# The first group's C and x0 inside the modulation stream, and the second modulation's sets one group later

## The reference

```python
mx = modulation(c, ada_w, ada_b)          # silu(c) @ ada_w + ada_b, split in 6 of 2048
hx = modulate(rms_norm(x, norm_g[0]), mx[0], mx[1])      # first modulation: shift, scale
yx, _ = ssd_mixer(hx, hc, w_in, conv_w, ..., w_out)      # hc: the same of ctx with c_ctx
x = x + mx[2] * yx
hx = modulate(rms_norm(x, norm_g[1]), mx[3], mx[4])      # second modulation
x = x + mx[5] * hier_moe(hx)              # top-1 group of 4, top-2 expert of 8

# ssd_mixer
z, xbc, dt = split(h @ w_in, [4096, 4096 + 6144])        # xbc: x 4096, B 1024, C 1024
xbc = silu(conv3(xbc)); dt = softplus(dt + dt_bias)      # 64 heads, two directions
# per direction: chunked scan, y = C (decays) B x, context first, then latent
y = rms_norm((y_fwd + y_bwd + d_skip * x) * silu(z), norm_g) @ w_out
```

## Time and profile before

| what | us |
|---|---|
| median of 3 runs (2125.37 to 2130.33) | 2125.74 |
| the profiled execution | 2125.82 |
| its span, first to last instruction | 2124.3 |
| TensorE busy | 1958.4 (92%) |
| VectorE busy | 1229.8 (58%) |
| ScalarE busy | 496.5 (23%) |
| GpSimd busy | 153.7 (7%) |
| DMA, mean over the span | 308 GB/s |

### The profile page before, as it was taken

One profiled execution on the slowest core, in us unless ns is written; L12 is line 12 of the kernel. 1 busy time (PEld: TensorE's weight loads), 2 busy tenths in 40 slices (PEclk: granted clock), 3 DMA queues, 4 the chain that ended last, 5 costly groups with the idle time before them and its releaser, 6 DMA issues.

```text
span 2124.3 us, 27901 instructions
## 1 busy us (share of the span) xinstructions
PE 1958.4 (92%) x10096; PEld 1213.4 (57%) x10097; DVE 1229.8 (58%) x2010; ACT 496.5 (23%) x577; POOL 153.7 (7%) x214
## 2 busy tenths in 40 slices
PE   5778999999999999999987999988999998899897
PEld 2357888888888888877876433333333333333332
DVE  2457898989999998988875433222332232333224
ACT  3233434343434243444443200000000000000000
POOL 0000010101000000002961000000000000000000
PEclk9789999999999999999998999999999999999999
DMA  9958577768686868596745699999999699999996
GB/s 360 317 162 266 173 237 213 240 182 267 183 256 179 255 188 249 174 334 244 257 165 218 275 426 428 425 426 425 427 429 425 255 426 426 425 428 426 425 427 274
DMA packets 293597, 654.10 MB, mean 308 GB/s; under 512 B 13408, under 2 KB 187904, under 8 KB 260912
## 3 DMA queue, kind: packets, MB, share of 16 engines
q1 hardware_dynamic: 284608, 626.86, 79.0%
q0 software_dynamic: 7984, 26.40, 3.8%
q10 hardware_dynamic: 960, 0.23, 0.1%
HBM read 642.81 MB, written 10.65 MB: 308 GB/s over the span
## 4 chain that ended last, share of the span: by engine, by line
DMA 27%; PE 19%; POOL 4%; DVE 1%; issue 1%; SPq 1%; ACT 0%; DVEq 0%; POOLq 0%
DMA wt<-in_moe_w_up 27%; PE bank L1875 13%; PE bank L1730 2%; POOL ysq L648 2%; POOL ysq L655 1%; PE bank L1900 1%; POOL ysq L653 1%; PE bank L1855 1%; SPq L536 1%; PE bank L1837 0%; PE bank L1838 0%; PE bank L1789 0%; PE bank L1782 0%; PE bank L1830 0%; DVE x L1502 0%
## 5 line engine op out<-in xcount | busy, mean ns | idle before, releaser
L1875 PE MATMUL bank<-wt,xe 128*64 128x512 f32 x1984 | 465.2, 624 | 75.8 <-DMA wt<-in_moe_w_up 75.8
L1502 DVE TENSOR_TENSOR x<-x,bank 128x512 f32<-128x512 f32 x256 | 158.5, 682 | 528.4 <-PE bank L1855 528.4
L1623 PE MATMUL bank<-hTh,whi 128*128 128x256 f32 (+1 forms) x1264 | 408.5, 343 | 9.5 <-ACT whi L716 6.6
L1624 PE MATMUL bank<-hTl,whi 128*128 128x256 f32 (+1 forms) x1264 | 401.9, 338 | 0.0
L1875 PEld LDWEIGHTS bank<-wt,xe 128*64 128x64 f32 x1984 | 162.7, 144 | 374.9 <-issue 374.9
L1623 PEld LDWEIGHTS bank<-hTh,whi 128*128 128x128 f32 x1264 | 242.9, 192 | 37.1 <-ACT whi L716 6.8
L1624 PEld LDWEIGHTS bank<-hTl,whi 128*128 128x128 f32 x1264 | 242.8, 192 | 24.1
L1630 PE MATMUL bank<-hTh,wlo 128*128 128x256 f32 (+1 forms) x1264 | 231.3, 336 | 0.9 <-DVE wlo L967 0.9
L1900 PE MATMUL bank<-wt,hdn 128*64 128x512 f32 x1024 | 226.8, 596 | 1.4 <-DVE hdn L1514 1.4
L879 ACT ACTIVATE gsb<-bank 128x512 f32<-128x512 f32 x32 | 19.1, 597 | 828.5 <-PE bank L1875 828.5
L1630 PEld LDWEIGHTS bank<-hTh,wlo 128*128 128x128 f32 x1264 | 196.9, 190 | 25.3 <-DVE wlo L967 1.1
(11 more groups left out here) (316 smaller groups left out, 1834.8 us busy)
## 6 DMA issues: line engine op xcount, KB each, us to landing
wt<-in_moe_w_gate SPq DMA_DIRECT2D x62, 2048.0 KB, 16.6
wt<-in_moe_w_up SPq DMA_DIRECT2D x62, 2048.0 KB, 21.1
wt<-in_moe_w_down SPq DMA_DIRECT2D x62, 2048.0 KB, 18.5
raw<-in_ssm_w_in SPq DMA_DIRECT2D x80, 1024.0 KB, 5.8
raw<-in_ada_w SPq DMA_DIRECT2D x70, 1024.0 KB, 6.1
raw<-in_ssm_w_out SPq DMA_DIRECT2D x32, 1024.0 KB, 5.1
fr<-in_ada_w SPq DMA_DIRECT2D x26, 1024.0 KB, 12.0
bc<-cum_d POOLq DMA_DIRECT2D x32, 512.0 KB, 5.3
```

Of the source, the lines that this page charges most:

```text
L1502: dve.tensor_tensor(x1[:, tt, cols], x1[:, tt, cols], banks[(1, 3, 6, 7)[nb]][:, :], ALU.add).then_inc(s_acc2, 1)
L1623: pe.matmul(bank[:, 0:width], wh[:, k, :], hTh[:, k, 0:width], start=(k == 0), stop=False)
L1624: last = pe.matmul(bank[:, 0:width], wh[:, k, :], hTl[:, k, 0:width], start=False, stop=False)
L1875: last = pe.matmul(banks[0][SLOTS * h:SLOTS * h + SLOTS, :], rows[:, k, :], wt[2 * q + h][:, FF * i:FF * i + FF], start=(k == 0), stop=(k ...
```

## The change

It has four parts.

**Slabs.** The front loads 36 tiles through eleven slots: 32 ada tiles and four slabs ("s", j). Slab j holds the quarter j of the rows of w_in for four chunks together: dt, B, C and x0 of group 0, as four DMAs of 256 KB. Each slab is converted once (`slab_hi`, `slab_lo`) and used by four parts, `part(j, c)`, of 12 matmuls each. The parts stand one by one between the ada blocks and turns. Block 1 stands between the transposes of x.

**Group 0** starts at chunk 3 (z0), has no ada tiles, and its dt chain is cut in two and spread over the steps. `c_times_b(0)` stands one step later, behind chunk 8.

**Sets one group back.** Group g sums the tiles of set g-1 (g = 1 to 7). The last eight tiles are loaded and summed in the output projection, at the places of DTILE, into rows of their own (`arow_d`), and their columns go to DRAM in a DMA of their own.

**GpSimd** computes the sum of squares for four chunks at once: 128x1024 per instruction, and two small sums at the end.

```diff
-    FSLOT = [0, 1, 2, 3, 4, 5, 6] * 2 + [7, 8, 3, 4, 5, 6, 7, 8, 3, 4, 5, 6, 7, 8, 4, 6, 7, 8, 4]
+    FTILES = [("a", i) for i in range(8)] + [("s", 0)] + [("a", i) for i in range(8, 12)] + [("s", 1)] + [("a", i) for i in range(12, 20)]
+    FTILES += [("s", 2)] + [("a", i) for i in range(20, 28)] + [("s", 3)] + [("a", i) for i in range(28, 32)]
+    FSLOT = [0, 1, 2, 3, 4, 5, 6, 0, 3, 1, 2, 4, 5, 6, 0, 3, 7, 8, 9, 10, 1, 2, 4, 5, 1, 0, 3, 7, 8, 1, 10, 4, 9, 2, 6, 0]
+    DTILE = (12, 14, 16, 18, 20, 22, 23, 25)
+    DLOADS = []
+    for i in range(NOT):
+        DLOADS += [("o", i)] + [("a", j) for j in range(NADA) if i == DTILE[j]]
...
@@ SP
             def front_free(pos):
-                if pos == DT_POS:
-                    sp.wait_ge(s_lo, 1)
+                kind, i = FTILES[pos]
+                if kind == "s":
+                    sp.wait_ge(s_lo, i + 1)
                     return
...
-            for i, (nb, q) in enumerate(OTILES):
+            for at_d, (kind, i) in enumerate(DLOADS):
...
+                if at_d < RAW:
+                    slot_free(GROUPS - 1, len(LOADS) - RAW + at_d)
+                elif DLOADS[at_d - RAW][0] == "o":
+                    sp.wait_ge(s_lo, M_OUT + DLOADS[at_d - RAW][1] + 1)
                 else:
-                    sp.wait_ge(s_lo, M_OUT + i - RAW + 1)
+                    sp.wait_ge(s_aadd, NADD * HLAST + ADDS[DLOADS[at_d - RAW][1]])
+                slot, _ = ring_d(kind, i)
+                if kind == "a":
+                    sp.dma_start(a_view(slot), ada_tile(2 * HLAST + NB1 + i // 4, i % 4)).then_inc(s_raw[slot], 16)
+                    continue
...
@@ GpSimd
-            for k in range(IC):
-                if k % GC == 0:
-                    pool.wait_ge(s_yld[k // GC], 32)
...
+            for g in range(GROUPS):
+                chunks = slice(GC * g, GC * g + GC)
+                pool.wait_ge(s_yld[g], 32)
+                if g > 0:
+                    pool.wait_ge(s_yss, g)
+                part = ysq[:, 1 if g == 0 else 0, :, :]
+                pool.tensor_tensor(part, yh[:, chunks, :].bitcast(F32), yl[:, chunks, :].bitcast(F32), ALU.add).then_inc(s_ysum, 1)
+                pool.wait_ge(s_ysum, g + 1)
+                if g == 0:
+                    pool.tensor_tensor(part, part, part, ALU.mult).then_inc(s_yss, 1)
+                    continue
+                pool.tensor_tensor(part, part, part, ALU.mult).then_inc(s_ysq, 1)
+                pool.wait_ge(s_ysq, g)
+                pool.tensor_tensor(ysq[:, 1, :, :], ysq[:, 1, :, :], part, ALU.add).then_inc(s_yss, 1)
...
@@ ScalarE
+            slab_hi(0)
             round_rows(0)
+            slab_hi(1)
             round_rows(1)
...
+                head = isinstance(g, int) and g == 0
+                if head:
+                    conv_hi(0, 4)
+                    act.wait_ge(s_du, 1)
+                    act.activation(dtw[:, 3, :], dtw[:, 2, :], ACT.Ln).then_inc(s_dln, 1)
+                    tanh_of(0, 0)
+                    conv_first(0, 2)
...
@@ VectorE
+            def ada_terms(row, tile, j, done):
+                for i in range(4):
+                    column = cvec[:, 4 * (j % 4) + i, 0:1]
+                    if j % 4 == 0 and i == 0:
+                        dve.tensor_scalar(row[:, :], tile[:, i, :], column, None, ALU.mult).then_inc(s_aadd, 1)
+                    else:
+                        dve.wait_ge(s_aadd, done + (4 * j + i))
+                        dve.scalar_tensor_tensor(row[:, :], tile[:, i, :], column, row[:, :], ALU.mult, ALU.add).then_inc(s_aadd, 1)
...
             ada_rows(0)
-            ada_rows(1)
             for k in range(0, KC, 2):
                 ...
+            ada_rows(1)
             modulated(0)
+            slab_lo(0)
             ada_rows(2)
+            slab_lo(1)
             ada_rows(3)
             modulated(1)
...
             for i in range(NCH, NOT):
                 out_lo(i)
+                if i - 1 in DTILE:
+                    ada_sum_d(DTILE.index(i - 1))
+                if i in (23, 28):
+                    ada_columns(GROUPS, i // 28)
+                if i == 29:
+                    dve.wait_ge(s_a2T, 2)
+                    dve.tensor_copy(a2row_d[:, :], ADAK[0:NADA, P:2 * P]).then_inc(s_a2r, 1)
...
@@ TensorE
+            PARTS = ((0, T), (1, T), (7, L), (4, T))
+            def part(j, c):
+                wh = whi[:, j % 2, :].rearrange("p (k c n) -> p k c n", k=4, c=4)
+                wl = wlo[:, j % 2, :].rearrange("p (k c n) -> p k c n", k=4, c=4)
+                bank, width = PARTS[c]
+                pe.wait_ge(s_lo, j + 1)
+                for i in range(4):
+                    k = 4 * j + i
+                    if c == 0:
+                        pe.wait_ge(s_hl, k + 1)
+                    pe.matmul(banks[bank][:, 0:width], wh[:, i, c, :], hTh[:, k, 0:width], start=(k == 0), stop=False)
...
+                if k % 4 == 3:
+                    ada_block(1, (k // 4,))
+            ada_turn(1)
+            ada_block(2)
+            part(0, 0)
+            ada_turn(2)
+            part(0, 1)
+            ada_block(3)
+            part(0, 2)
+            ada_turn(3)
+            part(0, 3)
...
+            ada_block(7)
+            part(2, 2)
+            ada_turn(7)
+            part(2, 3)
+            for c in range(4):
+                part(3, c)
...
-                    if w and n == 7:
+                    if w and n == (8 if head else 7):
                         c_times_b(g)
...
                 out_tile(i)
+                if i in (20, 26):
+                    ada_columns_d((i - 20) // 6)
+                if i == 28:
+                    pe.wait_ge(s_ads, 2 * GROUPS + 1)
+                    pe.transpose(ADAK[0:NADA, P:2 * P], adab[:, ADA1 + ADA2 - NADA:ADA1 + ADA2], ident[:, :]).then_inc(s_a2T, 1)
```

More of the change, by code:

```diff
@@ L454, in _ @@
                 front_load(pos)
[L455 to L464, removed]
-                else:
-                    front_free(max(q for q in range(FRONT) if FSLOT[q] == pos))
-                    return
+            for n in range(NSLAB, NCH):
+                slot, count = ring(0, "w", n)
+                if n < NSLAB + RAW:
+                    front_free(FLAST[slot])
+                else:
+                    sp.wait_ge(s_lo, n - RAW + 2)
+                sp.dma_start(w_view(raw, slot), w_in[:, :, bass.ds(w_in_at(0, n), P)]).then_inc(s_raw[slot], 16)
@@ L468, in slot_free @@
+            def slot_free(g, pos):
+                kind, n = LOADS[pos]
                 if kind == "w":
-                    sp.wait_ge(s_lo, NCH * bg + (n + 2))
+                    sp.wait_ge(s_lo, NCH * g + (n + 2))
                 else:
[L471 to L486, removed]
@@ L488, in _, with group_loads @@
-            group_loads(0, first=True)
-            with sp.Fori(1, GROUPS) as g:
+                    sp.wait_ge(s_aadd, NADD * g + (ADDS[n] - NADD))
+            def group_loads(g):
+                for pos in range(RAW, len(LOADS)):
+                    slot_free(g, pos - RAW)
+                    group_load(g, pos)
+            for pos in range(RAW):
+                sp.wait_ge(s_lo, NCH - RAW + pos + 2)
+                group_load(1, pos)
+            with sp.Fori(1, GROUPS - 1) as g:
                 group_loads(g)
+                for pos in range(RAW):
+                    slot_free(g, len(LOADS) - RAW + pos)
+                    group_load(g + 1, pos)
@@ L492, in y_load @@
+            group_loads(GROUPS - 1)
             def y_load(g, part):
@@ L1156, in steps @@
                 s = g - 1
-                for n in range(NCH):
+                head = isinstance(g, int) and g == 0
+                for n in range(4 if head else 0, NCH):
                     if ssd and w and n == 4:
@@ L1200, in steps @@
                         finish(s, 3)
-                    if w and n == 7:
+                    if w and not head and n == 7:
                         ada_columns(g, 0)
@@ L1736, in steps @@
                 s = g - 1
-                for n in range(NCH):
+                head = isinstance(g, int) and g == 0
+                for n in range(NSLAB if head else 0, NCH):
                     if not w and n == 0:
```

385 lines of the change are left out of this document (212 added, 173 removed).

## The result

The changed kernel takes 2166.89 us (median of 4 runs, 2166.27 to 2167.88), the kernel before, run beside it, 2126.59 (2125.37 to 2130.33): a ratio of 1.018, 95% interval 1.0167 to 1.0193. The forecast was 2174. The profiled execution has a span of 2165.4 us against 2124.3, 41.1 more. The two stages that the prediction priced explain it all: 26.0 us are gained before GpSimd's first operation, and 67.0 are lost from there to the last out tile.

A forecast was written before the change was run, and what follows sets the result against it. Loads bound the kernel to about 110 us, TensorE to 905 and in the output projection; expert-weight loads follow. 2125.8 - 21 (front, first group) + 69 (output projection) = 2174 us; range 2126 to 2192, the forecast's own 2158 to 2186.

The forecast's parts named there:

- +69: Output projection: last out tile would end at 1210 us against 1141, from GpSimd's longer operations and ada tiles sharing the ring.
- -21: Front and first group: the group would end at 208.6 us instead of 229.8, 21 us gained.
- Turns: Output projection: VectorE gets one operation per GpSimd operation, 2.75 us each, so out_lo takes 11 us per tile.
- The split rival: Output projection: VectorE and GpSimd split bandwidth, VectorE stays at 4.1 us per tile; +42, 2147 us; chance 0.18.
- The loop: Output projection: sum, issue of next ada and out tile, landing, ScalarE, out_lo, sum: 16.8 us per two tiles against TensorE's 10.9.
- The old stall: Output projection, tile 25: TensorE's wait for GpSimd, 6.3 us and 1.5 of half clock, would go.
- Group 0: First group after the front: 55.7 of chunks, 2.8 turns and C times B, 8 of new waits and half clock; 66.5 us.
- the wait of `c_times_b(0)`: Group 0: it follows x2 and needs dt_columns, which VectorE runs behind drain(0,8): 3.4 us, plus some 1.5 half clock.
- that of the first turn: Group 0: turn(0,0) needs the B conv, behind dt's exp and Ln on ScalarE: 1.5 us, plus some 1.5 half clock.
- The front: Before group 0: SP waits for slab 0 until 60 us, last ada tile lands at 124, front ends at 142 us.
- turns with the loads ready in time: Output projection rival: only the GpSimd chain costs, +33 less 8 of the old stall, +25; 2130 us; chance 0.08.
- The faster case: Rival: VectorE has room, the ring holds, the tile 25 wait goes; needs rounds under 12 us; 2098 us; chance 0.14.

The follow-up runs named there:

- e4: Changed kernel with two buffers of their own for the last ada set and SP's wait moved, GpSimd at 128x1024: 2130.6 us.
- e5: Changed kernel with one buffer of its own for the last ada set, SP waiting at the same place as in the changed kernel: 2171.7 us.
- e2: Changed kernel without the last eight ada tiles (loads, sums, column sums left out), GpSimd at 128x1024: 2124.0 us.
- e6: Changed kernel without the last ada set, GpSimd at 128x512: 2103.2 us.
- e3: Changed kernel without the last ada set and with GpSimd at 128x256; only front and group 0 differ from the kernel before: 2102.2 us.
- e7: Changed kernel with two own buffers for the last ada set, SP's wait moved, and GpSimd back at 128x256: 2108.6 us.
- e8: Two own buffers and GpSimd at 128x256, plus dt_columns moved ahead of drain(0,8) in group 0: 2107.6 us against 2108.6 without that move.
- e10: Two own buffers, 128x256, early dt_columns; four tiles of the last set moved to group 0, `ysq` read one tile later: 2097.9 us.
- e11: Last set halved between group 0 and output projection, own buffers, early dt_columns, later `ysq` read, but GpSimd at 128x512: 2108.8 us.
- e1: Changed kernel with GpSimd's operations back at 128x256, the last ada set still in the ring: 2145.8 us.

## Why the prediction was right

The direction, the two causes and the size came out of the walk: +69 forecast, 67.0 measured; -21 forecast, -26.0 measured. The two misses add to the 7 us by which 2174 was too high; they did not cancel. By its steps:

- **Turns.** 2.75 us per VectorE instruction forecast (its three terms give 2.71), 2.64 measured; the sum of a0 63.4 us after GpSimd's start, measured 61.7. The row that decided it was 1151.20 in the earlier trace rows. The Trainium skill (SBUF — State Buffer, Who interferes with whom) gives the rule that the two exclude each other. The traces agree at three sizes: VectorE's instruction takes 1.0 to 1.1, 1.63 and 2.64 us beside GpSimd operations of 256, 512 and 1024 elements. That is each time GpSimd's operation (0.61, 1.17 and 2.28 by the 2.18 ns per element) and some 0.4 more, which is less than the 0.69 that VectorE's takes alone, so the two overlap by some 0.3. The split rival is refuted by it: a split would have left VectorE at 1.04 at every size.
- **The loop.** 16.8 us a round forecast; measured, from the end of one sum to that of the next, 16.3, 16.4, 16.9 and 15.9 for a1 to a4. From the sum of a4 (1101.0) to the last out tile 81.1, forecast 80, a term that the prediction gives without its steps. e4 and e5 point to the order on SP: same work and same sums, 36 us less once SP's wait has already been passed when it comes, and nothing gained by the third slot alone.
- **The old stall** at tile 25 went, as the walk had it; it is gone in e2 and e6 as well, and back in e3.
- **Group 0.** 66.5 us forecast from the front's end, 65.7 measured (137.76 to 203.50); the wait of `c_times_b(0)` 3.4 forecast, 3.46 measured; that of the first turn 1.5 forecast, 0.71 measured.
- **The front was mis-sized**, 4 of the 5 us by which the gain was too small. I kept `modulated(0)` at 58.2 because its transposes are mixed with block 1; it ended at 55.9, so SP went on at 58.16 and not at 60, and the hole in the DMA queue was 2 us. The loads behind it then ran at 375 GB/s (62 to 118 us) and not at the 358 that I took from 40 to 60 us. So the last ada tile came at 120.4 instead of 124, and the front ended at 137.8 instead of 142. Another 0.9 of the 142 is a wrong addition: from 124, the steps up to the last hTl (1, 1.4, 1.1 and 6.0) make 133.5 and not 134.4. From the last tile to the front's end it was 17.3 us, and the terms give 17.0.

The other rivals: turns with the loads ready in time is what e4 made real, 2130.6 where the rival has 2130. The faster case needed rounds under 12 us; e7 comes nearest to it, 2108.6 against 2098, and it needed both causes removed. The front did not fail.

What is not settled: why e5 is 5 us over the changed kernel (its runs reach from 2165.3 to 2174.3), and what e8's edit is worth in time. Of e5's profiled execution, 7.4 us longer, the stage has only 1.4; 1.9 lie before it and 4.1 behind the last out tile, where the edit changes nothing.

## What to carry to other kernels

On an in-order DMA queue, a load that waits for a consumer holds up all loads behind it: give work woven into a tight stream buffers of its own, and put its loads where their wait has already been passed. Look at the length of GpSimd's operations beside a busy VectorE and not at their number: fewer and longer ones finished GpSimd 35 us earlier, and cost 21 us. And when a wait is taken away, ask what it was hiding: going from 256 to 512 cost 1 to 2 us while TensorE waited at tile 25 anyway (e3, e6), and 10 to 11 where it did not and sums came on top (e10, e11).

## What the runs showed of the hardware that was not expected

The front does not end at the same time in every execution. In some the last ada tile's matmuls (128x512, x8) take 1.06 us and the first turn comes at 143.9 to 145.0, in one at 145.8 (the changed kernel, e1, e7, e10 and e11, and e4). In others they take 1.93 and it comes at 147.5 to 148.4 (e2, e3, e5, e6, e8). The front's instructions are the same in all of them. The window of 118 to 126 us (busy us by engine, granted clock, DMA share, GB/s), of the changed kernel and then of e3:

```profile
118.00:126.00 8.00, 6.30 (x46) 4.35 (x39) 2.60 (x9) 0.67 (x2) 0.00 (x0) 1.00 0.96 267
```

```profile
118.00:126.00 8.00, 5.92 (x30) 3.35 (x31) 0.69 (x1) 0.00 (x0) 0.00 (x0) 0.59 0.81 224
```

The granted clock is 1.00, which is 2.4 GHz, in one. In the other it is 0.59 on average, most of the stretch at the lower level of 1.2 GHz; in e2, e5 and e8 it is 0.50 from 122 to 130 us. In e4 it fell only behind the last tile (0.58 from 122 to 130 us). TensorE has short waits for loads in front of the last tile in both kinds: 1.55 to 1.75 us where its matmuls took 1.06, 1.69 to 2.12 where they took 1.93. What tips it the one way or the other the runs don't show.

Part of it comes back. Where the front was late, C times B ran at 1.10 us instead of 1.58 to 2.04 after the same 3.46 us of waiting, and group 0 was 1.6 us shorter (53.9 against 55.5). At GpSimd's start 1 to 2 us are left (975.4 to 975.8 in e2, e3, e5 and e6 against 973.5 to 974.6 in the changed kernel, e1 and e7), as much as the 1.0 that e8's edit showed in the median.
